# Feed-forward activations of a hybrid encoder block: turned on TensorE, or on VectorE in 32x32 blocks with transfers inside SBUF

## What is computed

```python
def swiglu(x, w_gate, w_up, w_down):
    return (jax.nn.silu(x @ w_gate) * (x @ w_up)) @ w_down
...
h = h + 0.5 * swiglu(rms_norm(h, ffn1_norm[l]), ffn1_w_gate[l], ffn1_w_up[l], ffn1_w_down[l])
u = rms_norm(h, mix_norm[l]) @ w_in[l]
...                       # attention and RWKV-7 on u
h = h + jnp.concatenate([attn_out, rwkv_out], axis=-1) @ w_out[l]
h = h + 0.5 * swiglu(rms_norm(h, ffn2_norm[l]), ffn2_w_gate[l], ffn2_w_up[l], ffn2_w_down[l])
return rms_norm(h, final_norm)
```

## Time and profile before

| | us |
|---|---|
| median of 3 runs | 1940.38 (1940.26 to 1941.05) |
| the profiled execution, its own time | 1941.51 |
| its span, first to last instruction | 1939.6 |
| PE busy | 1908.5 (98%) |
| DVE busy | 1026.0 (53%) |
| ACT busy | 881.1 (45%) |
| DMA engines, mean busy share of the first DMA queue | 59.3% |

### The profile page before, as it was taken

One profiled execution on the slowest core, in us unless ns is written; L12 is line 12 of the kernel. 1 busy time (PEld: TensorE's weight loads), 2 busy tenths in 40 slices (PEclk: granted clock), 3 DMA queues, 4 the chain that ended last, 5 costly groups with the idle time before them and its releaser, 6 DMA issues.

```text
span 1939.6 us, 30763 instructions
## 1 busy us (share of the span) xinstructions
PE 1908.5 (98%) x11761; PEld 1624.1 (84%) x11761; DVE 1026.0 (53%) x1071; ACT 881.1 (45%) x1048; POOL 11.1 (1%) x23
## 2 busy tenths in 40 slices
PE   8999999999999999999999999999999999999997
PEld 7888888888888889999998878888888888888885
DVE  5454545455445454767566855445444455444543
ACT  6444444444444445745434655444444444434443
POOL 1000000000000000000000000000000000000000
PEclk9999999999999999999899999999999999999999
DMA  7666666666566667554333546766666666655553
GB/s 236 191 192 187 191 187 193 185 193 186 186 193 193 187 193 239 170 157 142 111 102 103 174 152 185 215 188 191 186 186 192 186 193 186 193 187 194 195 195 120
DMA packets 184093, 350.79 MB, mean 181 GB/s; under 512 B 13312, under 2 KB 15616, under 8 KB 183744
## 3 DMA queue, kind: packets, MB, share of 16 engines
q1 hardware_dynamic: 183232, 349.09, 59.3%
q10 hardware_dynamic: 256, 0.34, 0.1%
q0 software_dynamic: 512, 0.06, 0.0%
HBM read 345.24 MB, written 4.19 MB: 180 GB/s over the span
## 4 chain that ended last, share of the span: by engine, by line
PE 96%; DVE 1%; ACT 1%; issue 1%; DMA 0%; SPq 0%; ACTq 0%; DVEq 0%
PE psA L322 40%; PE psB L322 39%; PE psB L701 6%; PE psA L701 4%; PE psT L563 1%; PE psA L712 1%; DVE wlo L307 0%; DMA x<-in_x 0%; PE psM L1723 0%; PE psT L1103 0%; PE psM L1082 0%; PE psM L1710 0%; PE psT L390 0%; DVE lsum L1230 0%; PE psT L1734 0%
## 5 line engine op out<-in xcount | busy, mean ns | idle before, releaser
L307 DVE TENSOR_TENSOR wlo<-raw,whi 128x1024 fp32r<-128x1024 f32 (+1 forms) x648 | 789.0, 1219 | 837.6 <-ACT whi L298 823.3
L298 ACT CAST whi<-raw 128x1024 fp32r<-128x1024 f32 (+1 forms) x648 | 679.1, 1050 | 958.0 <-PE psA L322 434.3
L322 PE MATMUL psA<-whi,xh 128*128 128x512 f32 (+1 forms) x736 | 283.9, 386 | 0.0
L322 PE MATMUL psA<-wlo,xh 128*128 128x512 f32 (+1 forms) x736 | 283.4, 385 | 0.0
L322 PE MATMUL psA<-whi,xl 128*128 128x512 f32 (+1 forms) x736 | 283.4, 385 | 0.0
L322 PE MATMUL psB<-whi,xh 128*128 128x512 f32 x704 | 275.7, 392 | 0.0
L322 PE MATMUL psB<-whi,xl 128*128 128x512 f32 x704 | 274.0, 389 | 0.0
L322 PE MATMUL psB<-wlo,xh 128*128 128x512 f32 x704 | 274.0, 389 | 0.0
L322 PEld LDWEIGHTS psA<-whi,xl 128*128 128x128 f32 x736 | 138.5, 188 | 27.6
L322 PEld LDWEIGHTS psA<-whi,xh 128*128 128x128 f32 x736 | 138.6, 188 | 27.4
L322 PEld LDWEIGHTS psA<-wlo,xh 128*128 128x128 f32 x736 | 138.5, 188 | 27.5
(11 more groups left out here) (355 smaller groups left out, 2139.0 us busy)
## 6 DMA issues: line engine op xcount, KB each, us to landing
raw<-in_ffn_w_gate SPq DMA_DIRECT2D x176, 512.0 KB, 3.7
raw<-in_ffn_w_up SPq DMA_DIRECT2D x176, 512.0 KB, 3.7
raw<-in_ffn_w_down SPq DMA_DIRECT2D x176, 512.0 KB, 3.6
raw<-in_w_in SPq DMA_DIRECT2D x80, 512.0 KB, 3.6
raw<-in_w_out SPq DMA_DIRECT2D x32, 512.0 KB, 3.6
x<-in_x SPq DMA_DIRECT2D x4, 512.0 KB, 7.5
x_dram<-x SPq DMA_DIRECT2D x4, 512.0 KB, 8.6
x<-x_dram SPq DMA_DIRECT2D x4, 512.0 KB, 7.0
```

Of the source, the lines that this page charges most:

```text
L298: nc.scalar.copy(whi[:, slot, :, 0:ncol], raw[:, slot, :, 0:ncol]).then_inc(hi_ready, 1)
L307: nc.vector.tensor_tensor(wlo[:, slot, :, 0:ncol], raw[:, slot, :, 0:ncol], whi[:, slot, :, 0:ncol].bitcast(F32), ALU.subtract).then_inc(l ...
L322: mm = nc.tensor.matmul(ps[:, tb, 0:ncol], lhs[:, k0 + t, tok], rhs[:, slot, t, 0:ncol], start=(first and t == 0 and p == 0), stop=(last a ...
```

## The change

PE's `turn` goes, with its waits, and ACT and DVE no longer read `psT` in the feed-forward. In its place, for each of the 22 chunks:

- DVE turns `act` in 32x32 blocks within each group of 32 partitions (`turn_quads`, two instructions, one for each token block), behind `gate_up`, into the half of `stage` that holds `silu`, in the order in which the transfers want it.
- SP issues 16 transfers inside SBUF (`quads_move`), each of 32 partitions x 256 elements (1 KB a row, 32 KB in all): block row `src` of the source goes to the partitions 32 x `dst` of the destination, which is the half that holds `act`. They are placed two by two between the weight loads: the first pair, with a wait for `turn_quads`, behind the load of group 6, the last ahead of the load of group 13.
- ACT waits for all 16 ahead of `silu_gate(n)`, which now stands directly behind `whi` of group 11; the casts to `hh` are two instructions and stand behind `whi` of group 12. DVE's subtraction is two instructions behind `wlo` of group 13.
- PE keeps one wait ahead of the up groups, for `gate_up` of the chunk before (in the down stage, ahead of column block 1).

```diff
+        quads = silu.rearrange("p b c -> p (b c)").rearrange("p (q m h j) -> p h m q j", q=4, m=4, h=TB)
+        quads_out = silu.rearrange("p b c -> p (b c)").rearrange("p (q r) -> p q r", q=4)
+        quads_in = act.rearrange("p b c -> p (b c)").rearrange("p (a r) -> p a r", a=4)
+        landed = act.rearrange("p b c -> p (b c)").rearrange("p (a m h j) -> p h m a j", a=4, m=4, h=TB)
...
+        def quads_move(sp, f, n, a_):
+            if a_ == 0:
+                sp.wait_ge(quads_ready, n + (f * FC + 1))
+            for q in (2 * a_, 2 * a_ + 1):
+                src, dst = q // 4, q % 4
+                sp.dma_start(quads_in[32 * dst:32 * dst + 32, src, :], quads_out[32 * src:32 * src + 32, dst, :])\
+                    .then_inc(quads_landed, 16)
...
                 for j in range(SLOTS if f == 0 and isinstance(n, int) else 0, GD):
                     load_group(sp, rows(w_gate, j * KT)[:, :, bass.ds(col, COLS)], base, n, PER, j)
+                    if j >= 6 and not (isinstance(n, int) and n == 0):
+                        quads_move(sp, f, n - 1, j - 6)
                 for j in range(GD):
+                    if j < 6 and not (isinstance(n, int) and n == 0):
+                        quads_move(sp, f, n - 1, j + 2)
                     load_group(sp, rows(w_up, j * KT)[:, :, bass.ds(col, COLS)], base, n, PER, GD + j)
...
             def turned_hi(n):
-                nc.scalar.wait_ge(act_turned, n + (f * FC + 1))
-                nc.scalar.copy(hh[:, bass.ds(n * 4, 4), :], psT[:, :].rearrange("p (t s) -> p t s", t=4))\
-                    .then_inc(hh_ready, 1)
+                nc.scalar.wait_ge(quads_landed, n * 256 + 256 * (f * FC + 1))
+                for tb in range(TB):
+                    last = nc.scalar.copy(turned_tokens(hh, n, tb), landed[:, tb])
+                last.then_inc(hh_ready, 1)
...
                     if j == GD + SLOTS - 1:
                         if not first:
-                            turned_hi(n - 1)
+                            nc.scalar.wait_ge(quads_landed, n * 256 + 256 * f * FC)
                         silu_gate(n)
+                    if j == GD + SLOTS and not first:
+                        turned_hi(n - 1)
...
+            def turn_quads(n):
+                nc.vector.wait_ge(act_ready, n + (f * FC + 1))
+                for tb in range(TB):
+                    last = nc.vector.transpose(quads[:, tb], act[:, tb, :])
+                last.then_inc(quads_ready, 1)
...
                     if j == SLOTS - 1 and not first:
                         gate_up(n - 1)
+                        turn_quads(n - 1)
...
-                    elif j == GD + SLOTS - 1:
+                    elif j == GD + SLOTS + 1:
                         turned_lo(n - 1)
...
-            def turn(n):
-                nc.tensor.wait_ge(act_ready, n + (f * FC + 1))
-                if not (isinstance(n, int) and n == 0 and f == 0):
-                    nc.tensor.wait_ge(hl_ready, n + f * FC)
-                for t in range(4):
-                    for tb in range(TB):
-                        mm = nc.tensor.transpose(psT[:, t * S + tb * P:t * S + tb * P + P],
-                                                 act[:, tb, t * P:t * P + P], ident)
-                mm.then_inc(act_turned, 1)
...
                 if not first:
-                    turn(n - 1)
+                    nc.tensor.wait_ge(act_ready, n + f * FC)
```

More of the change, by code:

```diff
@@ L252, in build @@
         act_ready = sem("act_ready")
-        act_turned = sem("act_turned")
+        quads_ready = sem("quads_ready")
+        quads_landed = sem("quads_landed")
         hh_ready = sem("hh_ready")
@@ L412, in x_lo, with turned_tokens @@
             mm.then_inc(xl_ready, 1)
+        def quads_move(sp, f, n, a_):
[5 more added lines that the diff above has]
+                    .then_inc(quads_landed, 16)
+        def turned_tokens(arr, n, tb):
+            return arr[:, bass.ds(n * 4, 4), tb * P:tb * P + P].rearrange("p m (a j) -> p m a j", a=4)
         def ffn_load(sp, f, base, w_gate, w_up, w_down):
@@ L429, in ffn_load, with down_half @@
             down = base + FC * PER
-            with sp.Fori(0, DC // 2) as m:
+            def down_half(m, first):
                 for j in range(2 * GF):
+                    if first and 6 <= j < 14:
+                        quads_move(sp, f, FC - 1, j - 6)
                     col = (2 * m + j // GF) * COLS
                     load_group(sp, rows(w_down, (j % GF) * KT)[:, :, bass.ds(col, COLS)], down, m, 2 * GF, j)
+            down_half(0, True)
+            with sp.Fori(1, DC // 2) as m:
+                down_half(m, False)
         def ffn_act(f, base, first_act):
@@ L471, in ffn_act @@
                 split_hi(down, 0, 0, j)
-                if j == SLOTS + 1:
+                if j == GD + SLOTS:
                     turned_hi(FC - 1)
@@ L484, in gate_up @@
                 if not (isinstance(n, int) and n == 0 and f == 0):
-                    nc.vector.wait_ge(act_turned, n + f * FC)
+                    nc.vector.wait_ge(hl_ready, n + f * FC)
                 for tb in range(TB):
@@ L489, in gate_up @@
                 last.then_inc(act_ready, 1)
+            def turn_quads(n):
[3 more added lines that the diff above has]
+                last.then_inc(quads_ready, 1)
             def turned_lo(n):
                 nc.vector.wait_ge(hh_ready, n + (f * FC + 1))
-                nc.vector.tensor_tensor(hl[:, bass.ds(n * 4, 4), :], psT[:, :].rearrange("p (t s) -> p t s", t=4),
-                                        hh[:, bass.ds(n * 4, 4), :].bitcast(F32), ALU.subtract)\
-                    .then_inc(hl_ready, 1)
+                for tb in range(TB):
+                    last = nc.vector.tensor_tensor(turned_tokens(hl, n, tb), landed[:, tb],
+                                                   turned_tokens(hh, n, tb).bitcast(F32), ALU.subtract)
+                last.then_inc(hl_ready, 1)
             def chunk(n, first):
@@ L514, in ffn_dve @@
             gate_up(FC - 1)
+            turn_quads(FC - 1)
             for c in range(DC):
@@ L518, in ffn_dve @@
                         split_lo(down, 0, 0, c * GF + j)
-                    if not c and j == SLOTS + 2:
+                    if not c and j == GD + SLOTS + 1:
                         turned_lo(FC - 1)
@@ L599, in ffn_pe @@
             for c in range(DC):
+                if c == 1:
+                    nc.tensor.wait_ge(act_ready, (f + 1) * FC)
                 if c >= 2:
@@ L604, in ffn_pe @@
                         turn_x(1, c - 1)
-                    if c == 0 and j == 2:
-                        turn(FC - 1)
                     if c == 0 and j == (KF - 4) // KT:
```

## The result

| | before | after |
|---|---|---|
| median, us (range, runs) | 1940.32 (1939.55 to 1941.05, 4) | 1926.63 (1925.52 to 1927.16, 4) |
| ratio of the two, 95% interval | | 0.9929 (0.9912 to 0.9946) |
| profiled execution, its span | 1941.51, 1939.6 | 1927.16, 1925.3 |

The forecast was 1920.6 us in a range of 1919.3 to 1924.3 us. The changed kernel is faster, as forecast, but by 13.7 us and not by 19.8. In three later sessions it stood at 1924.83, 1924.83 and 1925.55 us beside 1940.21, 1941.62 and 1942.14 us of the kernel before: 15.4, 16.8 and 16.6 us faster. So 3 to 6 us of the forecast gain are missing.

A forecast was written before the change was run, and what follows sets the result against it. PE alone was taken to bound the feed-forwards. Removing 22 turns of 0.90 us, with all new work hidden, takes 19.8 us off 1940.4 us: 1920.6 us, in a range of 1919.3 to 1924.3 us.

The forecast's parts named there:

- What is removed: PE's turn in each of 22 chunks, all on the path: 0.90 us each, 19.8 us in all.
- DVE's block turns: Two 128x512 instructions behind `gate_up`, 0.69 us each; hidden from PE up to 2.9 us each.
- Rival 1: Slower: each DVE block turn takes 3.49 us, so PE waits at group 4; 1947.4 us, chance 0.03.
- SP's queue: Transfers issued between weight loads: group 7's load leaves at about 110.1 us, at 0.62 us an issue; no cost.
- Nothing waits: Group 7's load lands 3.7 us after issue, at 113.8 us, before ACT wants it.
- the cover that the text names: Slack before PE reads a group: 8.2 us after its slot is free, 5.8 us more of cover for late loads.
- The price is nothing at either end: SP's issues cost no time at 0.62 us or at 1.29 us each, the latter slipping 0.3 us a group.
- The landing: The last transfers land 2.6 us after issue, ahead of ACT's wait; hidden even at 10.7 us.
- Bandwidth: Sixteen 32 KB transfers a chunk take 0.12 us each, raising the DMA share from 0.65 to about 0.70.
- Rival 2: Slower: each small transfer holds the DMA engines 2.0 us, so loads set the pace; 2303 us, chance 0.04.
- The sum: Whole kernel: 19.8 us off the median of 1940.4 us gives 1920.6 us, all new work hidden.
- Rival 3: Part of the gain: an unseen wait or late landings hold PE within a chunk; half is 1930.5 us, chance 0.04.

The follow-up runs named there:

- e10: The changed kernel with an unused reciprocal of 128x1024 on DVE behind the block turns of the first feed-forward; 1950.67 us (one run).
- e9: The changed kernel with every SBUF transfer of the first feed-forward issued twice on SP, the second into an unused buffer; 1952.59 us.
- e13: The changed kernel with a second set of the first feed-forward's SBUF transfers, issued on POOL's (GpSimd's) queue; 1926.30 us.
- e12: The kernel before the change with 104 tiny turns added at the start of PE's program; 1955.60 us beside 1942.14 us without them.
- e1: The changed kernel with 24 tiny PE turns without a reader added in the first down stage; 1925.47 us.
- e3: The changed kernel with 20 float32 matmuls of 512 columns and 4 tiny turns, all without a reader, in the first down stage; 1939.08 us.
- e5: The changed kernel with 24 tiny turns added at the very start of PE's program; 1924.33 us.
- e11: The changed kernel with 24 tiny turns in the mixing step, where PE waits for ACT and DVE; 1920.97 us.
- e2: The changed kernel with three float32 matmuls without a reader in the first feed-forward's chunk loop, run 9 times; 1943.31 us.
- e4: The kernel before the change with PE's turns and the waits for them left out, nothing in their place (wrong activations); 1927.30 us.
- a3: The changed kernel itself, measured again in a later session; 1924.83 us beside 1941.62 us of the kernel before.
- e7: The changed kernel with 128 tiny turns added at the very start of PE's program; 1938.67 us.
- e6: The changed kernel with 64 tiny turns added at the very start of PE's program; 1928.13 us.

## Why the prediction was wrong, point by point

The sign, the place and the size of the gain in the feed-forwards were right; the time lay 2.3 us above the range. By the prediction's own parts:

- **What is removed.** Forecast 0.90 us a turn. Measured: a chunk of 43.52 us for 44.42. The lead is 9.79 us at the end of the first feed-forward and grows by 9.00 us over the chunks of the second. Those are 10.9 and 10.0 turns at 0.90 us, 21 of the 22; one lies behind it, in the last down stage. Right.
- **DVE's block turns.** Forecast 0.69 us in 0.48 to 3.49; measured 0.691. The limit at which they would cost was borne out by e10. Rival 1 fell.
- **A rule of the Trainium skill.** "VectorE: DVE Perf Modes", its rules for kernel authors, would leave a 128x128 transpose to TensorE. The trace speaks against it for this kernel: the chunk is 0.90 us shorter with the turns on DVE, as PE alone bounds it.
- **SP's queue.** Forecast: the load of group 7 at about 110.1 - 103.73 = 6.4 us into the chunk, with two issues of 0.62 us. Measured 109.53 - 102.94 = 6.6 us, and 0.58 us an issue. But its claim "Nothing waits" was off: that load was there 5.2 us after its issue (114.75 - 109.53) and not 3.7, and held ACT 0.9 us longer than PE does. In the median, loads of w_gate land in 4.2 us and of w_up in 4.6, where line 287 had 3.6 us before. It stayed hidden in the cover that the text names. And "The price is nothing at either end" was wrong at the dear end: the text reckons a slip of 0.3 us a group for issues of 1.29 us, and counts five groups, without the four issues ahead of group 8 (4 x 1.29 + 0.4 = 5.6 us for a group of 2.72). e9, in effect two issues of 1.2 us ahead of a load and four ahead of group 8, has that slip (3.08 - 2.72 = 0.36 us) and is 27.8 us slower than the changed kernel. This did no harm, as an issue took 0.58 us, but the bound was not safe.
- **The landing.** Forecast 2.6 us; measured 1.8 to 5.6, 3.8 us in the median. Hidden, as forecast; in e9, where SP issues the last pair late, it is there that the cover gives out.
- **Bandwidth.** Forecast a share of 0.70; measured 0.69. Rival 2 fell, by e13 even for twice the transfers.
- **The sum.** This is the step that failed. It took 22 x 0.90 us off the time of the whole kernel, and so took it as given that the stages between, whose instructions the change does not touch, keep their length. The mixing step got 5.46 us longer in the profiled execution (475.31 us for 469.86), 2.57 us of it a stop for PE's own program, the rest stretches at half clock less the waits that went. The range had 0.1 us a chunk "for something small between two stages", 2.2 us, where 3 to 6 us were needed. Rival 3 spoke of a part of the gain, but sought the loss in new waits within a chunk; it was not there.
- **The cause**, as far as it is shown: removing code ahead of the mixing step moves the borders of the pieces in which PE's program is loaded, so that a border falls behind the 169th of 248 short turns and PE stops for 2.6 us (e12 shows it in the kernel before, e1, e3, e5 and e11 undo it, e2 and e4 exclude the time and the new work). In each of the eleven the clock is at half for 3.4 to 6.8 us at the stop, and e1, e3 and e5 have no such stretch there. What is not shown is why the other two stretches at half clock, near 794 and 1135 us, come more often with it: nine of the eleven have one or both; a3 and e7 have neither, and theirs are the two shortest of these mixing steps (472.81 and 473.64 us); of the seven without the long stop only e1 has one. The stretch near 794 us lies ahead of the stop in time, so the stop cannot be what brings it.

With the code put back in an idle place (e11), the gain is 21.2 us, 1.4 us more than the 19.8 of the forecast; the reckoning of the feed-forwards holds, and the rest is within what sessions differ by.

## What to carry to other kernels

Before the gain of one stage is booked for the whole kernel, list the stages behind it whose program moves in memory, and look in them for long rows of very short instructions on the engine that bounds them; a few us belong in the range for each. If an untouched stage changes its length, move the code by some instructions that compute nothing needed, placed in an idle stretch, before any cause is sought in the data. For work moved to a DMA queue, compare the issue time ahead of each load with the period of the loads (here 2 x 0.58 + 0.4 us against 2.72 us), and leave room, since e9's durations came to 2.7 us and its period to 3.08; here it is the queue's issuing engine, not the bandwidth, that gives out first.

## What the runs showed of the hardware

- PE's program comes in pieces of 16.4 KB (67 of them in 1.9 ms), a border every 128 turns of 32x32 with their weight loads. At 16 ns a turn such rows outrun the loads: PE goes on 2.2 to 2.6 us after a load begins, and stands 2.4 to 2.8 us with the border behind the 169th turn, 1.8 us behind the 233rd, 0 to 0.6 us behind the 145th. A second such row stops for 2.6 us in the kernel before as well.
- At such a stop the granted clock fell to 0.50 for 3.4 to 6.8 us; at e6's of 1.80 us it did not, and at e11's of 0.58 us it did. A stretch of 3.4 us cost 1.4 to 1.7 us.
- An issue of a 32 KB transfer inside SBUF takes SP 0.58 us (0.51 to 0.62), one of a 512 KB load from memory 0.38 to 0.40 us. A 32 KB transfer lands in 3.8 us in the median beside those loads.
- DVE turns 128x512 float32 in blocks of 32x32 in 0.691 us, no more than an operation with two inputs of that size; its reciprocal of 128x1024 takes 6.51 us.
- A float32 matmul of 512 columns is two matmuls on PE and takes 0.85 us, back to back, against 0.227 us for the fp32r ones of the same size (e3).
